# The opening of a two-block transformer kernel: the first modulation in three pieces, and the first weight strip among its loads

## The reference, cut to what matters

```
cond = silu(c)
mod = cond @ w_mod[l] + b_mod[l]                  # (1024) @ (1024 x 9216)
sh1, sc1, g1, sh2, sc2, g2, sh3, sc3, g3 = jnp.split(mod, 9, axis=-1)
h = rms_norm(x, norm_g[l, 0]) * (1.0 + sc1) + sh1
x = x + 0.5 * g1 * swiglu(h, w_ffn1_gu[l], w_ffn1_down[l])
```

## Time and profile before

| what | value |
|---|---|
| median of three runs | 1761.39 us (1760.89 to 1761.67) |
| profiled execution: span from first to last instruction | 1759.8 us |
| TensorE busy in it | 1732.4 us (98%) |
| VectorE, ScalarE, GpSimd busy | 1419.2, 1006.7, 184.0 us |
| read from memory | 438.38 MB |
| mean granted TensorE clock | 0.999 |

### The profile page before, as it was taken

How to read it: one execution, slowest core, us unless ns; L and a number is a source line. 1 busy time by engine, 2 the same in 40 slices (tenths; PEclk the granted TensorE clock), 3 DMA queues, 4 the chain that set the end, 5 groups by cost and what they waited for, 6 DMA issues and landing times.

```text
span 1759.8 us, 24720 instructions
## 1 busy us (share of the span) xinstructions
PE 1732.4 (98%) x9178; PEld 1470.0 (84%) x9178; DVE 1419.2 (81%) x2185; ACT 1006.7 (57%) x1666; POOL 184.0 (10%) x382
## 2 busy tenths in 40 slices
PE   6999999999999999999999999999999999999998
PEld 3888888888888888988888888888888888888886
DVE  7899987898899888878888866579888876688565
ACT  5445577755475556877545644556455544465454
POOL 3021012111111111021110000001110000010000
PEclk9999999999999999999999999999999999999999
DMA  9999742699869985418898654459886483466551
GB/s 352 356 360 393 273 147 83 259 332 337 315 225 340 332 314 205 168 51 317 329 334 291 224 206 158 161 191 333 324 325 249 169 301 146 185 229 245 204 194 70
DMA packets 125144, 441.10 MB, mean 251 GB/s; under 512 B 15248, under 2 KB 18272, under 8 KB 124896
## 3 DMA queue, kind: packets, MB, share of 16 engines
q1 hardware_dynamic: 91024, 316.17, 49.1%
q0 software_dynamic: 33296, 120.12, 18.2%
q10 hardware_dynamic: 704, 3.23, 0.5%
HBM read 438.38 MB, written 1.09 MB: 250 GB/s over the span
## 4 chain that ended last, share of the span: by engine, by line
PE 94%; DVE 2%; DMA 2%; ACT 1%; issue 1%; SPq 0%; DVEq 0%; ACTq 0%
PE banks L2368 24%; PE banks L2169 15%; PE banks L2373 12%; PE banks L2147 11%; PE banks L2174 7%; PE banks L2152 6%; PE banks L2317 2%; PE banks L2321 2%; PE banks L2326 2%; PE banks L2137 1%; PE banks L2139 1%; PE banks L2138 1%; DMA weights_raw<-in_w_mod_first 1%; PE banks L2281 1%; DVE weights_lo L1355 1%
## 5 line engine op out<-in xcount | busy, mean ns | idle before, releaser
L1355 DVE TENSOR_TENSOR weights_lo<-weights_raw,weights_hi 128x1024 fp32r<-128x1024 f32 (+2 forms) x584 | 685.9, 1200 | 67.5 <-ACT weights_hi L810 66.7
L810 ACT ACTIVATE weights_hi<-weights_raw 128x1024 fp32r<-128x1024 f32 (+2 forms) x584 | 584.8, 1036 | 68.3 <-PE banks L2174 21.9
L2368 PE MATMUL banks<-hT,weights_hi 128*128 128x512 f32 x1856 | 464.1, 392 | 0.0
L2368 PEld LDWEIGHTS banks<-hT,weights_hi 128*128 128x128 f32 x1856 | 337.3, 189 | 63.0
L2373 PEld LDWEIGHTS banks<-hT,weights_lo 128*128 128x128 f32 x1856 | 253.2, 190 | 18.1
L1368 DVE CUSTOM_DVE_ANT_0 arena<-arena,mod_acc,vectors 128x1024 f32<-128x1024 f32 x216 | 267.6, 1280 | 0.0
L2373 PE MATMUL banks<-hT,weights_lo 128*128 128x256 f32 x1856 | 258.8, 282 | 0.0
L1004 ACT ACTIVATE arena<-banks 128x512 f32<-128x512 f32 x116 | 69.3, 598 | 323.1 <-PE banks L2373 322.9
L2147 PE MATMUL banks<-weights_hi,hT 128*128 128x512 f32 (+2 forms) x896 | 218.2, 385 | 0.0
L2147 PEld LDWEIGHTS banks<-weights_hi,hT 128*128 128x128 f32 x896 | 165.6, 188 | 29.9
L1690 DVE TENSOR_TENSOR arena<-banks,arena 128x512 f32<-128x512 f32 x116 | 79.8, 688 | 108.9 <-ACT arena L1004 108.9
(11 more groups left out here) (358 smaller groups left out, 1971.3 us busy)
## 6 DMA issues: line engine op xcount, KB each, us to landing
weights_raw<-in_w_ffn_gu SPq DMA_DIRECT2D x176, 512.0 KB, 4.5
arena<-in_w_mod POOLq DMA_DIRECT2D x128, 512.0 KB, 6.2
weights_raw<-in_w_in SPq DMA_DIRECT2D x104, 512.0 KB, 4.1
weights_raw<-in_w_ffn_down SPq DMA_DIRECT2D x88, 512.0 KB, 5.0
arena<-in_w_ada POOLq DMA_DIRECT2D x88, 512.0 KB, 5.6
weights_raw<-in_w_ffn_in SPq DMA_DIRECT2D x88, 512.0 KB, 4.1
weights_raw<-in_w_ffn_out SPq DMA_DIRECT2D x44, 512.0 KB, 4.5
weights_raw<-in_w_out SPq DMA_DIRECT2D x32, 512.0 KB, 3.8
```

The source lines that it names most:

```text
L810: nc.scalar.activation(whi[:, n % PARTS, 0:width], raw[:, slot, 0:width], ACT.Copy).then_inc(S("hi_done"), credit(n))
L1355: V.tensor_tensor(wlo[:, n % PARTS, 0:width], raw[:, n % RING, 0:width], whi[:, n % PARTS, 0:width].bitcast(F32), ALU.subtract).then_inc(S ...
L2368: T.matmul(half_banks(j)[:, kind, :], whi[:, n % PARTS, 256 * k + P * kind:256 * k + P * (kind + 1)], hx[:, :, 4 * q + k, :], start=q == 0 ...
```

## The change

The first modulation (16 units as before, the same bytes, laid out anew by `first_units`) is cut into three pieces by blocks of 128 columns: piece 0 is eight units with blocks 0 to 3 of scale and shift, piece 1 four units with blocks 4 and 5, piece 2 four units with blocks 6 and 7. A unit of pieces 1 and 2 holds two row blocks of half the width, so it takes sixteen matmuls of 128 columns. Each piece is summed in its own bank and stored with its scale columns at once. The first strip is written out among the units. The loads of its four weight units move ahead of the last modulation units; strip 1's first four units move ahead of the constants and gains. Reduction 3 and reach 4 of the window bias move from ahead of the first strip into the stretch behind it; a bias pass uses three banks in place of four. ScalarE takes over seven of the eight scalings of x, and all row scalings. GpSimd makes the low parts of the first strip's units 1 and 2, before its loads. The warming matmuls go.

```diff
+MOD_PIECES = ((0, 8, 0, 4), (8, 4, 4, 2), (12, 4, 6, 2))
+PIECE_BANKS = (3, 4, 5)
+BIAS_BANKS = ((5, 6, 7), (0, 1, 7))
...
@@ sync
-            for m in range(MOD_FIRST_UNITS):
+            for m in range(0, 10):
                 mod_load(sp, m)
-            sp.wait_ge(S("mod_read"), 6)
-            gu_strip(RING, phases[0][2]["gu"], 0, (0,))
+            sp.wait_ge(S("mod_read"), reads_to(5))
+            first_weight(0)
+            first_weight(1)
+            for m in range(10, 12):
+                mod_load(sp, m)
+            sp.wait_ge(S("mod_read"), reads_to(6))
+            first_weight(2)
+            for m in range(12, 16):
+                mod_load(sp, m)
             sp.wait_ge(S("mod_summed"), 1)
-            gu_strip(RING, phases[0][2]["gu"], 0, (1,))
+            first_weight(3)
...
-                        sp.wait_ge(S("mod_summed"), 2)
+                        sp.wait_ge(S("mod_summed"), len(MOD_PIECES))
+                        gu_strip(n0 + 4, a["gu"], 1)
                         sp.dma_start(con[:, C_MASKW:], A["con"][:, C_MASKW:]).then_inc(S("const_loaded"), 16)
...
-                        gu_strip(c, a["gu"], b)
+                        if n0 > RING or b > 1:
+                            gu_strip(c, a["gu"], b)
@@ gpsimd
+            def lo_static(n):
+                pool.wait_ge(S("hi_done"), n + 1)
+                pool.wait_ge(S("lo_done"), n)
+                G.tensor_tensor(wlo[:, n % PARTS, :], raw[:, n % RING, :], whi[:, n % PARTS, :].bitcast(F32), ALU.subtract).then_inc(S("lo_done"), 1)
...
             angles()
+            lo_static(RING + 1)
+            lo_static(RING + 2)
             pool.wait_ge(S("hi_done"), RING + PREFETCH)
@@ scalar, first_phase
-                hi_static(RING, SLOT)
-                act.wait_ge(S("scale_ready"), 1)
-                act.wait_ge(S("mod_stored"), 2)
-                x_scaled(a, 0, True, (1,))
+                act.wait_ge(S("mod_stored"), 1)
+                x_scaled(a, 0, True)
                 x_hi(0)
                 x_scaled(a, 1, True)
                 x_hi(1)
-                act.wait_ge(S("mod_stored"), 3)
+                hi_static(RING, SLOT)
+                x_scaled(a, 2, True)
+                x_hi(2)
+                x_scaled(a, 3, True)
+                x_hi(3)
                 hi_static(RING + 1, SLOT)
-                x_hi(2)
-                x_hi(3)
-                hi_static(RING + 2, SLOT)
+                act.wait_ge(S("mod_stored"), 2)
                 x_scaled(a, 4, True)
                 x_hi(4)
+                x_scaled(a, 5, True)
+                x_hi(5)
+                hi_static(RING + 2, SLOT)
                 hi_static(RING + 3, SLOT)
-                x_hi(5)
+                act.wait_ge(S("scale_ready"), 1)
                 x_scaled(a, 6, True)
                 x_hi(6)
-                x_scaled(a, 7, True)
                 x_hi(7)
@@ vector, phase 1 (after x_stats, reaches 0 to 2 and reductions 0 and 1)
+                    piece_store(0, a)
+                    bias_take(2)
                     x_low(0)
+                    x_low(1)
                     lo_static(n0, SLOT)
...
                     x_low(2)
                     x_low(3)
-                    lo_static(n0 + 2, SLOT)
+                    bias_reach(3)
+                    piece_store(1, a)
                     x_low(4)
-                    x_scaled(a, 5, first=True)
-                    lo_static(n0 + 3, SLOT)
                     x_low(5)
+                    dve.wait_ge(S("mod_stored"), 2)
+                    piece_store(2, a)
+                    dve.wait_ge(S("scale_ready"), 1)
+                    x_scaled(a, 7, first=True)
                     x_low(6)
                     x_low(7)
+                    dve.wait_ge(S("lo_done"), n0 + 3)
+                    lo_static(n0 + 3, SLOT)
...
                     if f == 0:
-                        bias_reach(5)
+                        units(n0 + 4, n0 + 5)
+                        bias_take(3)
+                        units(n0 + 5, n0 + 6)
+                        bias_reach(4)
...
                     gated(0)
...
-                        units(c + 2, c + 4)
-                        mod_units(mod_slot(f, b))
+                        units(c + 2, c + 3)
                         if f == 0 and b == 1:
                             bias_take(4)
+                            bias_reach(5)
+                        units(c + 3, c + 4)
+                        mod_units(mod_slot(f, b))
                         act_lo(b - 1)
                         units(c + 4, c + 6)
                         if f == 0 and b == 1:
                             bias_take(5)
@@ tensor
+                    mod_unit(7)
+                    x_turn(1, (0, 1), 1)
+                    bias_pass(2)
+                    mod_unit(8)
+                    mod_unit(9)
+                    pe.wait_ge(S("bias_taken"), 3)
+                    x_turn(0, (2, 3), 1)
+                    x_turn(1, (2, 3), 1)
+                    pe.wait_ge(S("mod_stored"), 1)
+                    opening_high(n0, 0, hhi, "hhi_done")
+                    opening_high(n0, 0, hlo, "hlo_done")
+                    mod_unit(10)
+                    mod_unit(11)
+                    opening_low(n0, 0)
+                    opening_high(n0, 1, hhi, "hhi_done")
+                    opening_high(n0, 1, hlo, "hlo_done")
+                    mod_unit(12)
+                    mod_unit(13)
+                    opening_low(n0, 1)
+                    mod_unit(14)
+                    opening_high(n0, 2, hhi, "hhi_done")
+                    mod_unit(15)
+                    opening_high(n0, 2, hlo, "hlo_done")
+                    opening_low(n0, 2)
+                    bias_pass(3)
+                    opening_high(n0, 3, hhi, "hhi_done")
+                    opening_high(n0, 3, hlo, "hlo_done")
+                    opening_low(n0, 3)
...
                         gate_up(c, 2, 3)
+                        gate_up(c, 3, 4)
                         if f == 0 and b == 1:
                             bias_pass(5)
                             pe.wait_ge(S("const_loaded"), 32)
-                        gate_up(c, 3, 4)
-                        if f == 0 and b == 1:
                             pe.wait_ge(S("bias_taken"), 6)
                         down(c + 4, b - 1)
```

More of the change, by code:

```diff
@@ L85, with piece_of, ends_piece, reads_to @@
 HALF_STEPS = {"cross": (5, (1, 4)), "silu": (5, (2, 5)), "hi": (5, (3,)), "sum": (4, (1, 3)), "made": (4, (2, 4))}
+def piece_of(m):
+    return sum(m >= first + units for first, units, _, _ in MOD_PIECES)
+def ends_piece(m):
+    return any(m == first + units - 1 for first, units, _, _ in MOD_PIECES)
+def reads_to(m):
+    return sum(not ends_piece(i) for i in range(m + 1))
 def made_by_rows(f):
@@ L471, in x_block @@
             if pair == 0 and k == 1:
-                return (1, 384) if first else (5, 256)
-            if pair == 3 and k == 1 and first:
-                return 0, P
+                return (0, P) if first else (5, 256)
             b, c0 = (X_AT_FIRST if first else X_AT)[pair]
@@ L525, in mod_load @@
                 if same:
-                    eng.wait_ge(S("mod_read"), same[-1] - same[-1] // 8 + 1)
+                    eng.wait_ge(S("mod_read"), reads_to(same[-1]))
             elif on_pe(was):
-                eng.wait_ge(S("mod_summed"), was // 8 + 1)
+                eng.wait_ge(S("mod_summed"), piece_of(was) + 1)
             else:
@@ L870, in norm_stage @@
                 root(k, 0)
-                for c0, c1 in ((0, 256), (512, 1024)):
-                    scale_x(0, c0, c1, "xn0_ready")
+                scale_x(0, 0, 256, "xn0_ready")
+                if k == 1:
+                    scale_x(0, 256, 512, "xn1a_ready")
+                scale_x(0, 512, 1024, "xn0_ready")
                 if after is not None:
@@ L880, in norm_stage @@
                 root(k, 1)
+                if k == 1:
+                    scale_x(1, 0, 256, "xn1a_ready")
+                    scale_x(1, 256, 512, "xn1a_ready")
                 scale_x(1, 512, 1024, "xn1b_ready")
@@ L1402, in bias_take @@
                 dve.wait_ge(S("bias_summed"), q + 1)
-                for g in range(4):
-                    c = P * (q // 2) + 64 * (q % 2) + 16 * g
-                    ins = V.tensor_reduce(bias[:, :, c:c + 16], bank[g + (4 if q < 4 else 0)][:, 0:288].rearrange("p (k q h) -> p h k q", q=3, h=WH), AX, ALU.add)
+                for g in range(3):
+                    c, n = P * (q // 2) + 64 * (q % 2) + 24 * g, (24, 24, 16)[g]
+                    ins = V.tensor_reduce(bias[:, :, c:c + n], bank[BIAS_BANKS[q // 3][g]][:, 0:18 * n].rearrange("p (k q h) -> p h k q", q=3, h=WH), AX, ALU.add)
                 ins.then_inc(S("bias_taken"), 1)
@@ L1479, in x_low @@
                 x_is_scaled(dve, scales[0], g)
-                if g == 0:
-                    dve.wait_ge(S("scaled_by_dve"), 4 * (scales[0] - 1) + 1)
+                if g == 0 and scales[0] > 1:
```

(41 more changed lines are left out.)

145 lines of the change are left out of this document (57 added, 88 removed).

## The result

The changed kernel takes **1772.59 us** (median of 4 runs, 1772.38 to 1773.97) against 1761.53 for the kernel before on the same chip (4 runs). The ratio is 1.0063, 95% interval 1.0051 to 1.0076: 11 us slower. The profiled execution spans 1770.3 us, before 1759.8, so it shows 10.5 us of the loss.

A forecast was written before the change was run, and what follows sets the result against it. TensorE, busy for 98% of 1759.8 us, was taken to bound the kernel. Late down weights start the first down unit at 63.9 instead of 58.48, 5.4 us lost: 1761.4 + 5.4 = 1766.8 us, range 1761.5 to 1770.0.

The forecast's parts named there:

- First strip (24.4 to 43.0): The opening on TensorE: the first strip starts near 24.4 instead of 32.6 and ends at 43.0, 2.6 us before 45.6.
- The exclusion: VectorE and GpSimd shut each other out in the first strip: GpSimd's first subtraction ends at 31.8; without it 1.7 us less.
- VectorE's chain (59.4): VectorE's work from the last low part to the last bias reduction ends at 59.4 at best, where it was 58.42.
- 18.5 us of work: VectorE's work from 40.9 us to the last bias reduction, with a subtraction (1.2), reduction 3 (1.5) and reach 4 (2.3) added.
- rival (a): Down units land by 55 us, VectorE alone sets the first down unit's start: 59.5, +1.0, 1762.4 us; chance 0.22.
- The gains: Five small loads ahead of the down pair on SyncE's queue: they lose 0.8 us of queue, between 0 and 2.7.
- The even split: SyncE's and GpSimd's queues share evenly, as between 42 and 58 us before: 3.08 and 3.36 MB, full engines.
- The down pair: The two down units' loads, last on SyncE's queue behind all 7.97 MB: the second lands at 59.9.
- 2.0 + 19.7 + 0.8: Time to the second down unit's landing: issue to first byte, 7.97 MB at full rate, and the loss in the gains.
- Behind the landing: 1.05 + 1.2 + 1.5 + 0.2: After 59.9: ScalarE 1.05, VectorE's subtraction 1.2, reduction 1.5, hops 0.2, so TensorE starts the first down unit at 63.9.
- The clock, rival (c): TensorE comes back slow after its wait ahead of the first down unit: 2 us on top of the forecast, 1768.8; chance 0.12.

The follow-up runs named there:

- the three runs with the loads out of the way: The changed kernel with constants and gains behind strip 2's down pair (1765.39 us), both ahead of the third piece's wait (1765.40), or GpSimd's six rows held (1765.81).
- the run with both late: The changed kernel with constants and gains both moved behind strip 2's down pair: 1765.39 us, ratio 1.0026.

## Why the prediction was right about the sign and wrong about the size

The forecast was right in its mechanism: late down weights behind constants, gains and GpSimd's rows, ending in a reduction that follows two subtractions. It gave +5.4 us; +11.1 was measured, outside the range. Three terms of its sum were wrong: the gains (0.8, measured 2.5), what follows the landing of the down weights (3.95, measured 5.0), and the clock (nothing, measured 2.1). By its steps, in the profiled execution:

- **First strip (24.4 to 43.0).** 23.38 to 41.7. All of it was right in kind and ran 0.9 to 1.4 us early: the reach ended at 28.3, not 29.2, and the last sum came at 36.0 (35.34 + 0.64), not 37.4. The exclusion is there as I took it. The Trainium skill, "SBUF — State Buffer", "SBUF: two separate sides", says that the port pair which the two engines share is locked for a whole instruction and that the loser blocks; a VectorE operation takes part in this if it has two inputs in SBUF or runs in a 2-port mode. The trace agrees: 28.3, the reach's end, + 2.39 is 30.7, and the subtraction ended at 30.6, while the operation at 28.21 that reads a bank kept its 0.28 us.
- **VectorE's chain (59.4).** 59.3 to 60.1 in the three runs with the loads out of the way. The number is right, the way to it only in part, which is luck. In the run with both late the low parts ended at 39.1 instead of 40.9, so 18.5 us of work would have ended at 57.6; on top came VectorE's wait of 2.26 us for strip 1's first weights, which the sum ("at best") did not have. Those runs became rival (a), though at +3.5 to +3.9 us in the median instead of +1.0: a unit 0.9 to 1.6 us late, and mostly the slow clock behind its gap. The one profiled execution of them in which the clock did not fall took 1763.26, +1.3.
- **The gains: "between 0 and 2.7 I take 0.8, near the lower end because both queues together ran at the full rate".** This step failed, in its size. From 50.4 to 59.3 us 291 GB/s moved instead of 404: 8.9 x (1 - 291/404) = 2.5 us lost. The even split of the earlier trace rows held for two streams of large packets. Here the split was even in packets, not in bytes: 354 each from 50 to 54 us, 0.11 MB of SyncE's against 1.31 of GpSimd's. The Trainium skill, "DMA: Bandwidth & Descriptors", "Queues, rings and completion order", says that each DMA engine takes turns between the queues that have work, and switches only after a whole packet. The counts agree with it, although the page calls a group of descriptors a packet, which need not be what the profile counts. The run with GpSimd's rows away (3.4 instead of 8.8 us) fits it too.
- **The down pair.** The second landed at 41.44 + 20.06 = 61.5; I had 59.9. From 36.05 that is 25.4 us, 2.9 more than my 2.0 + 19.7 + 0.8. The gains explain 1.7; 388 instead of 404 GB/s from 38 to 50.4 us another 0.5. The remaining 0.7 I can't place.
- **Behind the landing: 1.05 + 1.2 + 1.5 + 0.2.** I had the first unit of the pair made before the second landed. ScalarE waits for one semaphore of both, so VectorE had two subtractions (2.36) to do: 66.47 - 61.5 = 5.0 instead of 3.95. This step failed too.
- **The clock, rival (c).** Given a chance of 0.12 as a case of its own, it came with the forecast: 2.1 us, where I took 2. That the sizes agree is luck: the 2 was picked between 0 and half of 10.3 us, and the slow row at 8.48 that gave these bounds has a granted clock of 1.00 in the profile (8.3 to 9.6 us). The Trainium skill, "TensorE: Matmul & The Clock Gate", "HAM oscillation", says that a TensorE that waits for DMA is throttled again and starts its next burst slow, and the trace agrees (0.51 behind 9.3 us of waiting). This step failed in the sum: a consequence of the forecast was left out of it as a case of its own.

The sum: 5.4 - 1.4 + 2.9 + 1.0 = 7.9 against 8.0 at the first down unit, + 2.1 for the clock = 10.1, of 10.5 in the span. The rest, 0.4 behind the unit and 0.6 between the profiled span and the medians, I leave.

## What to carry to other kernels

A step that is moved takes its place in every queue: ask what else is under way when its small loads come up. 0.17 MB of short packets beside another queue's bulk rows held their own queue for 8.8 us; in the empty stretch just before they were as good as out of the way altogether (1765.40 against 1765.39 us). Work pulled forward on TensorE pays only if the engine next in line is freed by as much: the gain came when VectorE's reach and reductions followed. And if a forecast is a wait, the clock behind the wait belongs into its sum.

## What was not expected of the hardware

- An idle time of 2.58 us on TensorE was followed by full speed in one execution (1.17 us a group) and by a granted clock of 0.57 in another (1.51, then 1.91), with the same work ahead of it. Of the five profiled executions with an idle time of 2.5 to 2.6 us there, the clock fell in four. After 1.63 us it stayed at 1.00 in the execution profiled.
- In one execution the clock was 0.79 from 30 to 38 us, the order of two DMA queues turned around, and the second strip started 4.4 us later (47.34 against 42.89). Half a us between two waits on different engines decided that order. Another execution met it with the clock at 1.00, and its second strip started at 47.37.
- A VectorE addition of four columns took 1.73 us beside GpSimd's subtraction of 1024 columns, and 0.17 in the run without that subtraction. An operation of 128 columns that reads a bank, 0.6 us earlier, was not held.
